# One-hots of the second expert index made token by token with partition scalars, and two weight remainders moved to VectorE

## The reference

```
q = (xt @ w_query).reshape(T, 8, 2, 128)          # two half queries per head
s_half, i_half = top_k(scores of both halves, 16)
top_s, pos = top_k(all sums of a first and a second half, 16)
ids = i_half[first] * 128 + i_half[second]         # expert (i, j) of 128 x 128
gates = softmax(top_s)
a = gelu(u_tab[ids] . x)                           # 128 experts a token
y = sum(gates * a * v_tab[ids])
```

## Time and profile before

| | us |
|---|---|
| median of 3 runs | 3461.05 (3458.17 to 3468.78) |
| the profiled execution | 3455.95 |
| its span | 3454.1 |
| PE busy | 3315.2 |
| DVE busy | 2983.2 |
| ACT busy | 2189.5 |
| POOL busy | 1302.3 |

### The profile page before, as it was taken

The page is one execution under the profiler, slowest core; times in us unless marked ns, Lnnn a source line. Parts: engine busy times, 40 slices in busy tenths (PEclk is TensorE's granted clock), DMA queues, the critical chain, the costliest instruction groups (busy, mean ns, idle before and its releaser), DMA issues.

```text
span 3454.1 us, 62688 instructions
## 1 busy us (share of the span) xinstructions
PE 3315.2 (96%) x19278; PEld 2433.7 (70%) x19278; DVE 2983.2 (86%) x6039; ACT 2189.5 (63%) x3116; POOL 1302.3 (38%) x1126
## 2 busy tenths in 40 slices
PE   6999999999999999999999999999999999999999
PEld 5777775667777767777777677766666777677777
DVE  6899877999888888888879997789988887888888
ACT  4574425557777677777746724455677776677777
POOL 0000017306555645555500000271255555556554
PEclk9999999999999999999999999999999999999999
DMA  5312263459999999999922123535699999999998
GB/s 201 104 58 71 92 256 104 154 180 327 365 362 342 341 364 360 361 351 358 337 90 88 56 80 122 213 117 177 213 326 346 356 338 349 366 364 355 359 354 303
DMA packets 421657, 868.79 MB, mean 252 GB/s; under 512 B 167824, under 2 KB 233360, under 8 KB 421008
## 3 DMA queue, kind: packets, MB, share of 16 engines
q1 hardware_dynamic: 310512, 544.87, 46.4%
q0 software_dynamic: 73728, 268.47, 21.4%
q10 hardware_dynamic: 37152, 52.45, 4.1%
HBM read 774.41 MB, written 85.98 MB: 249 GB/s over the span
## 4 chain that ended last, share of the span: by engine, by line
PE 43%; issue 26%; DVE 15%; POOL 10%; ACT 2%; DMA 2%; POOLq 0%; DVEq 0%; SPq 0%; ACTq 0%
PE ps L927 9%; PE ps L930 9%; PE ps L931 9%; POOL gbuf L589 6%; POOL spare L603 4%; PE ps L639 3%; PE ps L641 3%; PE ps L640 3%; DVE yT L1506 3%; DVE i L1752 2%; DVE v L1748 1%; DMA raw<-stream 1%; PE ps L673 1%; PE ps L674 1%; DVE S_ring L1758 1%
## 5 line engine op out<-in xcount | busy, mean ns | idle before, releaser
L673 PE MATMUL ps<-h,w 128*128 128x384 f16 (+1 forms) x2272 | 757.9, 334 | 34.0 <-ACT w L1015 33.2
L674 PE MATMUL ps<-h,w 128*128 128x384 f16 (+1 forms) x2272 | 754.7, 333 | 0.0
L1015 ACT ACTIVATE w<-w_hi 128x1024 f16<-128x1024 f32 x544 | 572.4, 1052 | 265.8 <-DVE w L1934 150.0
L603 POOL TENSOR_TENSOR spare<-spare 128x1 f32<-128x1 f32 x504 | 370.7, 735 | 908.7 <-DVE a_sp L1740 488.3
L930 PE MATMUL ps<-cf,w 128*128 128x384 f16 x2032 | 663.4, 327 | 0.0
L931 PE MATMUL ps<-cf,w 128*128 128x384 f16 x2032 | 660.7, 326 | 0.0
L670 PE MATMUL ps<-h_hi,w_hi 128*128 128x384 f32 (+1 forms) x2272 | 490.0, 357 | 0.0
L927 PE MATMUL ps<-cf_hi,w_hi 128*128 128x384 f32 x2032 | 428.4, 353 | 7.0 <-DVE cf L1928 7.0
L1934 DVE SCALAR_TENSOR_TENSOR w<-raw,w_hi 128x1024 f16<-128x1024 f32 x256 | 313.0, 1223 | 128.9 <-ACT w_hi L1010 99.6
L670 PEld LDWEIGHTS ps<-h_hi,w_hi 128*128 128x128 f32 x2272 | 396.1, 189 | 17.5 <-issue 0.3
L1003 ACT ACTIVATE w_hi<-raw 128x1024 fp32r<-128x1024 f32 x296 | 313.6, 1059 | 144.8 <-DMA raw<-stream 104.1
(11 more groups left out here) (285 smaller groups left out, 6227.4 us busy)
## 6 DMA issues: line engine op xcount, KB each, us to landing
raw<-stream SPq DMA_DIRECT2D x682, 512.0 KB
gelu_scratch<-g_out ACTq DMA_DIRECT2D x256, 192.0 KB
cg<-gelu_scratch SPq DMA_DIRECT2D x256, 192.0 KB
c_scratch<-stage SPq DMA_DIRECT2D x128, 256.0 KB
cg<-c_scratch SPq DMA_DIRECT2D x256, 128.0 KB
qT<-ada SPq DMA_DIRECT2D x32, 512.0 KB
cgate<-ada SPq DMA_DIRECT2D x32, 512.0 KB
w_rows<-ada SPq DMA_DIRECT2D x32, 512.0 KB
```

The costliest lines, as they stand in the source:

```text
L603: nc.gpsimd.tensor_tensor(spare[:, 16:17], spare[:, 17:18], spare[:, 18:19], ALU.add).then_inc(room, 1)
L673: nc.tensor.matmul(ps[:, b, 0:n], w16[:, s, 0, c], h16[:, c, 1, t0:T], start=False, stop=False)
L674: mm = nc.tensor.matmul(ps[:, b, 0:n], w16[:, s, 1, c], h16[:, c, 0, t0:T], start=False, stop=c == C - 1)
L1015: nc.scalar.mul(w16[:, s, 1], w_hi[:, s].bitcast(F32), X_DOWN).then_inc(w16_done, 1)
```

## The change

Three things. The j one-hots of a group are no longer made as a cube and multiplied: for each of the 8 tokens and each of the two gate parts, one DVE `tensor_scalar` compares a 128-column f16 row of numbers with the token's index, a per-partition f32 scalar, and multiplies by the gate, a second per-partition f32 scalar (16 instructions of 128 columns in place of three of 1024; the i one-hot stays). For this, indices and gates of j are kept in f32, a 128-column f16 row of numbers is made once at the start, and the gated tiles are stored token by token, so that PE reads them without gaps. The gate step of each 128 tokens gets two more instructions. Second, the remainders of query tiles 68 and 69 are made by DVE, after it has updated chunk 7 and before the second norm; POOL's first `low16` is then that of tile 70. Third, ACT's half words of tiles 68 and 69 stand behind the root in its queue. The semaphore between one-hot and gating goes, and the constants in POOL's waits follow.

```diff
--- before.py
+++ after.py
@@ -217,7 +217,8 @@
         cosT = keep("cosT", [P, T])
         sinT = keep("sinT", [P, T])
         ident16 = keep("ident16", [P, P], F16)
-        cur[0] += 960 - 256
+        iota16 = keep("iota16", [P, P], F16)
+        cur[0] += 960 - 512
         rstd_base = cur[0]
         rstd = keep("rstd", [P, T])
         sq_base = cur[0]
@@ -279,9 +280,11 @@
         esum = at("esum", base + 47 * KB, [P, 2, NB, RH])
         row_no = at("row_no", small + 6784, [P, 2, P])
         routed = at("routed", small + 8192, [P, NB, 3, RH * TOPK])
-        ij = at("ij", base + 64 * KB, [P, 2, ND], F16)
-        gate_hi = at("gate_hi", base + 64 * KB + 1536, [P, ND], F16)
-        gate_lo = at("gate_lo", base + 64 * KB + 2304, [P, ND], F16)
+        i_pick = at("i_pick", base + 64 * KB, [P, ND], F16)
+        j_pick = at("j_pick", base + 64 * KB + 768, [P, ND])
+        gate_hi = at("gate_hi", base + 64 * KB + 2304, [P, ND])
+        gate16 = at("gate16", base + 64 * KB + 3840, [P, ND], F16)
+        gate_lo = at("gate_lo", rstd_base, [P, ND])
         g_out = at("g_out", base + 68 * KB + 512, [P, 2, ND])
         sparse = base + 71 * KB + 512
         ids_u = at("ids_u", sparse, [P, P], U32)
@@ -291,9 +294,8 @@
         stage = at("stage", base, [P, 2, NKEYS, HALF])
         keys = at("keys", base + 74 * KB, [P, 2 * RH, NKEYS])
         one_i = at("one_i", base + 74 * KB, [P, 2, GROUP // 2, P, 2], F16)
-        one_j = at("one_j", base + 78 * KB, [P, 2, GROUP // 2, P, 2], F16)
-        gated_hi = at("gated_hi", base + 82 * KB, [P, 2, GROUP // 2, P, 2], F16)
-        gated_lo = at("gated_lo", base + 86 * KB, [P, 2, GROUP // 2, P, 2], F16)
+        gated_hi = at("gated_hi", base + 78 * KB, [P, 2, GROUP, P], F16)
+        gated_lo = at("gated_lo", base + 82 * KB, [P, 2, GROUP, P], F16)
 
         cg = at("cg", base + 74 * KB, [P, 4, NS + ND])
         coef = at("coef", base + 84 * KB, [P, 2, ND])
@@ -418,7 +420,6 @@
         id_r = sem("id_r")
         numbered = sem("numbered")
         gate_high = sem("gate_high")
-        j_done = sem("j_done")
         h_tr = sem("h_tr")
         h_ev = sem("h_ev")
         ids_in = sem("ids_in")
@@ -557,7 +558,7 @@
                 def low16(s, i):
 
                     high = pool.snap(l * NT + i + 1)
-                    up = pool.snap(l * (C * 2 + U_POOL) + i - I_QRY + 1)
+                    up = pool.snap(l * (C * 2 - 2 + U_POOL) + i - I_QRY - 1)
                     pool.wait_ge(hi_done, high)
                     nc.gpsimd.tensor_tensor(raw[:, s], raw[:, s], con[:, K_UP:K_UP + 1].rearrange("p (o q) -> p o q", o=1)
                                             .broadcast_to([P, C, P]), ALU.mult).then_inc(raw_up, 1)
@@ -569,10 +570,8 @@
                 nc.gpsimd.tensor_tensor(spare[:, 19:20], spare[:, 17:18], spare[:, 18:19], ALU.add)
 
                 nc.gpsimd.memset(uT[:, :, 0:PAD], 0.0).then_inc(pad0, 1)
-                pool.wait_ge(lo_done, l * NT + I_QRY + 4)
+                pool.wait_ge(lo_done, l * NT + I_QRY + 6)
                 nc.gpsimd.tensor_tensor(spare[:, 15:16], spare[:, 17:18], spare[:, 18:19], ALU.add)
-                low16(0, I_QRY)
-                low16(1, I_QRY + 1)
                 for c in range(C):
                     pool.wait_ge(hhi_done, (2 * l + 1) * C + c + 1)
                     nc.gpsimd.tensor_tensor(h16[:, c, 1], h_hi[:, c].bitcast(F32), con[:, K_ONE:K_ONE + 1].broadcast_to([P, T]),
@@ -895,9 +894,9 @@
                         for t in range(4):
                             two, k = 2 * q + t // 2, t % 2
                             cols = ps[:, 2 + (2 * g + q) % 4, t * P:(t + 1) * P]
-                            nc.tensor.matmul(cols, one_i[:, g % 2, two, :, k], gated_hi[:, g % 2, two, :, k],
+                            nc.tensor.matmul(cols, one_i[:, g % 2, two, :, k], gated_hi[:, g % 2, 4 * q + t],
                                              start=True, stop=False)
-                            mm = nc.tensor.matmul(cols, one_i[:, g % 2, two, :, k], gated_lo[:, g % 2, two, :, k],
+                            mm = nc.tensor.matmul(cols, one_i[:, g % 2, two, :, k], gated_lo[:, g % 2, 4 * q + t],
                                                   start=False, stop=True)
                         mm.then_inc(c_mm, 1)
 
@@ -1220,11 +1219,11 @@
                     if i == I_OUT + 2:
                         act.wait_ge(tile_done, l * NT + I_OUT + 4)
                         act.dma_start(keys[:], keys_d[ll]).then_inc(key_in, 16)
-                half_word_at(I_QRY)
                 updated_square(C - 1)
-                half_word_at(I_QRY + 1)
                 act.wait_ge(sq_used, l + 1)
                 token_root(7)
+                half_word_at(I_QRY)
+                half_word_at(I_QRY + 1)
                 modulated(1)
 
                 def half_scores_in(hp):
@@ -1324,6 +1323,7 @@
             for n, (counter, start) in enumerate(starts):
                 nc.vector.memset(spare[:, n:n + 1], 0.0).then_inc(counter, start)
             dve.wait_ge(rope_in, 32)
+            nc.vector.tensor_copy(iota16[:], iota)
             nc.vector.tensor_copy(numbers[:], iota.rearrange("k (n o) -> k n o", o=1).broadcast_to([P, P, 2])).then_inc(numbered, 1)
 
             steps = [0]
@@ -1698,6 +1698,11 @@
                                                        op0=ALU.add, op1=ALU.mult).then_inc(x_scaled, 1)
                         dve.wait_ge(x_scaled, l + 1)
                         nc.vector.tensor_scalar(gs[:, 1], gs[:, 1], X_UP, None, ALU.mult).then_inc(lay, 1)
+                for i in (I_QRY, I_QRY + 1):
+                    dve.wait_ge(hi_done, l * NT + i + 1)
+                    nc.vector.scalar_tensor_tensor(out=w16[:, i % 4, 0], in0=raw[:, i % 4], scalar=W_UP,
+                                                   in1=w_hi[:, i % 4].bitcast(F32), op0=ALU.mult,
+                                                   op1=ALU.subtract).then_inc(lo_done, 1)
                 norm(1)
 
 
@@ -1875,10 +1880,12 @@
                 for tt in range(1, NB):
                     dve.wait_ge(rt_tr, l * NBD + tt)
                     cols, gate = slice(P * (tt - 1), P * tt), ps[:, 2 + tt, 2 * P:3 * P]
-                    nc.vector.tensor_scalar(gate_hi[:, cols], gate, GATE_UP, None, ALU.mult).then_inc(gate_high, 1)
-                    nc.vector.tensor_copy(ij[:, :, cols], ps[:, 2 + tt, 0:2 * P].rearrange("k (c t) -> k c t", c=2))
+                    nc.vector.tensor_scalar(gate16[:, cols], gate, GATE_UP, None, ALU.mult).then_inc(gate_high, 1)
+                    nc.vector.tensor_copy(i_pick[:, cols], ps[:, 2 + tt, 0:P])
+                    nc.vector.tensor_copy(j_pick[:, cols], ps[:, 2 + tt, P:2 * P])
                     dve.wait_ge(gate_high, l * NBD + tt)
-                    nc.vector.scalar_tensor_tensor(out=gate_lo[:, cols], in0=gate, scalar=GATE_UP, in1=gate_hi[:, cols],
+                    nc.vector.tensor_copy(gate_hi[:, cols], gate16[:, cols])
+                    nc.vector.scalar_tensor_tensor(out=gate_lo[:, cols], in0=gate, scalar=GATE_UP, in1=gate16[:, cols],
                                                    op0=ALU.mult, op1=ALU.subtract).then_inc(rt_ev, 1)
                 dve.wait_ge(rt_ev, (l + 1) * NBD)
                 cube = [P, GROUP // 2, NKEYS, 2]
@@ -1891,13 +1898,13 @@
                     while lows[0] <= min(group_tile(g) + 1, NKEYS - 1):
                         u_low()
                     dve.wait_ge(c_mm, l * 2 * GROUPS + 2 * g + 2)
-                    nc.vector.tensor_tensor(one_j[:, g % 2], in_pairs.broadcast_to(cube), spread_out(ij[:, 1], g),
-                                            ALU.is_equal).then_inc(j_done, 1)
-                    nc.vector.tensor_tensor(one_i[:, g % 2], in_pairs.broadcast_to(cube), spread_out(ij[:, 0], g), ALU.is_equal)
-                    dve.wait_ge(j_done, l * GROUPS + g + 1)
-                    nc.vector.tensor_tensor(gated_hi[:, g % 2], one_j[:, g % 2], spread_out(gate_hi, g), ALU.mult)
-                    nc.vector.tensor_tensor(gated_lo[:, g % 2], one_j[:, g % 2], spread_out(gate_lo, g),
-                                            ALU.mult).then_inc(lr_done, 1)
+                    nc.vector.tensor_tensor(one_i[:, g % 2], in_pairs.broadcast_to(cube), spread_out(i_pick, g), ALU.is_equal)
+                    for gated, gates in ((gated_hi, gate_hi), (gated_lo, gate_lo)):
+                        for t in range(GROUP):
+                            n = GROUP * g + t
+                            ins = nc.vector.tensor_scalar(gated[:, g % 2, t], iota16[:], j_pick[:, n:n + 1], gates[:, n:n + 1],
+                                                          ALU.is_equal, ALU.mult)
+                    ins.then_inc(lr_done, 1)
                     while dots[0] < dots_by(g + 1):
                         dot()
                 while lows[0] < NKEYS:
```

## The result

| | before | after |
|---|---|---|
| median, us | 3459.6 (4 runs) | 3560.2 (3557.7 to 3563.5, 4 runs) |
| span of the profiled execution, us | 3454.1 | 3556.1 |

The ratio is 1.0278, 95% interval 1.026 to 1.0296: +96 us, +90 to +102. The forecast was 3535 us with a range of 3492 to 3600. The direction, the stage and the price of the new instruction held; a quarter of the loss was not in the sum.

What follows compares the result with a forecast made beforehand. PE was taken to bound the group stages, DVE having 1.1 to 1.3 us a group spare. Groups +78, gate step +1.3, row of numbers +0.2, norm -5.6: +74 on 3455.95, 3530; as median 3535 us, range 3492 to 3600.

Steps and rivals of the forecast that it cites:

- DVE becomes the bound of the group stage: Group stages: 16 short instructions, 3.58 us, replace 1.81, +1.78 us a group, more than DVE's spare time; together +78 us.
- the residual idle time, 9 us a layer: Group stages: idle time DVE would still have once it is the bound, added to the sum as 9 us a layer.
- the 2.1% of the first u tiles: DVE's idle share at 660 to 770 us, where it sets the pace; taken over for the group stages.
- rival B: Group stages: the ring DVE, PE, ACT, DVE keeps half of today's 110 us idle; +37 us, 3572 us, chance 0.10.
- the ring: Group stages: DVE, PE, ACT's copies and high part, DVE's remainder; 3.6 us around against 3.4 us of DVE work.
- PE's work stays at 382.7 us: Layer 1 group stage: PE's busy time of 382.7 us was to stay under 430, leaving PE room.
- Hidden up to 1.1 us a group, and beyond that DVE sets the end: Group stages: added DVE time up to 1.1 us a group costs nothing; beyond that, DVE sets the end.
- The second norm: With POOL quiet, DVE's four adds end sooner, chunk 7 is updated 2.8 us earlier, remainders nearly free; -5.6 us in all.
- rival D: Second norm: the change there gives nothing; 3541 us, inside the main case (0.60), with no chance of its own.
- A: Rival, group instructions: f16 gives at most two columns a cycle, step 0.258 us; +127 us, 3588 us, chance 0.17.
- C: Rival, group instructions: scalars hidden or short instructions cheaper, step 0.106 us, PE stays the bound; -4 us, 3457, chance 0.10.
- The gate step: Two PSUM reads and a cast replace one cast on DVE: +0.21 us three times a layer, +1.3 us in all.

Runs made afterwards that it cites:

- e5: The changed kernel with the gate of each token-wise instruction as a constant, leaving one partition scalar: 3495.7 us, ratio 1.0084 to the kernel before.
- e6: The changed kernel with both scalars of the token-wise instructions as constants, leaving out routing and gating: 3453.1 us, ratio 0.9964 to the kernel before.
- e7: The changed kernel comparing an f32 row of numbers in place of the f16 one: 3597.1 us, ratio 1.0383 to the kernel before.
- e4: The changed kernel with DVE's next remainder behind the group's dots instead of ahead of the group: 3527.4 us, ratio 1.0175 to the kernel before.
- e1: The kernel before with only the second norm's part changed (DVE's two remainders, half words behind the root): 3455.5 us, ratio 0.9972.
- e3: The kernel before, POOL starting its two remainders only after DVE's fourth add of squares, half words behind the root: 3456.4 us, ratio 0.9969.
- e8: e1 (groups as cubes) with the remainder order of e4: 3451.5 us, ratio 0.9964 to the kernel before.
- e2: The changed kernel with the second norm's part put back, leaving the groups' part alone: 3563.3 us, ratio 1.0281 to the kernel before.

## Why the prediction was right, and where it was short

- **DVE becomes the bound of the group stage: right.** The three numbers it was built from held: a fixed part of 0.07 us, 0.06 us a partition scalar, and 0.033 us for 128 f16 columns in place of 0.067 (e5, e6, e7). DVE's work came out at 420.0 us for 421.7.
- **The term that was too small: the residual idle time, 9 us a layer.** It was 23.2 and 17.5 us, 23 us more in all. From the sum's 74 us to the 102 between the two spans: +23 from this idle time, -4 from DVE's work, +9 from the rest of the kernel. The time is off by 25 and not by 28 because I added 5 us from the profiled execution to the median, and the changed kernel's is only 2 below its own. I took the 2.1% of the first u tiles, where DVE paces the kernel without such a ring. It was rival B's mechanism that came, given 0.10 and +37 us, and not half of the idle time stayed but 41 of 111 us. e4 takes it out and gets 35 us back, with 1.5% and 2.3% idle left, so 2.1% was about right for a DVE without the ring. That PE's work stays at 382.7 us did not hold either (395.6): the sum had no term for PE's clock falling where PE waits.
- **"Hidden up to 1.1 us a group, and beyond that DVE sets the end": wrong as a threshold.** From DVE's work, stage length and idle time of the group stages of layers 1 and 2, in us, one profiled execution each:

| kernel | step | DVE's work | stage | idle |
|---|---|---|---|---|
| e6 | 0.103 | 330.2, 330.1 | 387.6, 386.2 | 57.4, 56.1 |
| before | cubes | 338.0, 338.2 | 389.5, 397.4 | 51.5, 59.2 |
| e1 | cubes | 338.0, 337.9 | 394.2, 390.4 | 56.2, 52.6 |
| e5 | 0.164 | 375.2, 374.7 | 413.0, 408.7 | 37.8, 33.9 |
| after | 0.223 | 420.0, 419.9 | 443.2, 437.5 | 23.2, 17.5 |
| e7 | 0.256 | 444.6, 444.2 | 466.1, 455.3 | 21.5, 11.1 |

  From the kernel before to e5, 74 us of work in the two layers cost 35 us, though 111 were idle. Between kernels with the same cubes a stage differs by up to 7 us, so a single layer shows this only roughly, and whether the 8 us a layer between e6 and the cubes cost anything is not told: the stages say 11 to 13 us for both layers, the times of e6 and e1 are alike.
- **The second norm: right in mechanism.** -5.6 forecast, -7.1 by the traces' stretches, -10 (-6 to -14) by e1, so rival D (the norm gives nothing) is out. Chunk 7 came 2.7 and 2.1 us earlier where 2.8 was said; the surplus lies in PE's short steps behind it, which ran at a higher granted clock than before. Tile 67 was next, as said, and the remainders ended with the root (521.69 after 521.58). e3 shows the cause.
- **Rivals.** A is priced by e7: had the row of numbers run at two columns, +133 us (127 forecast). C (scalars hidden) falls with e5 and e6: its own step, 0.106, is what the instruction takes without scalars, and then the loss is gone, as it said. By the figure in the Trainium skill, "VectorE: DVE Perf Modes", section on the TRN2 errata, an instruction of this shape takes an estimated 94 ns, which is within a tenth of e6's 0.103 us and less than half of the 0.223 with two partition scalars.
- **The rest**: beside the stages' 94 us, the two spans differ by -1.6 ahead of the first group, +6.4 from the last group of layer 1 to the first of layer 2, and +3.6 behind. 1.8 in each of the last two is the last group's own instructions. The gate step took 1.1 us of it by the traces (1.3 forecast). What is left isn't explained by either part. From the last group of layer 1 to the first output chunk of layer 2 it is 1015.9 us in the kernel before and 1025.2 in the changed one, but 1019.9 to 1024.9 in e1, e3 and e8, which leave the groups as they were: the profiled execution of the kernel before was quick there.

## What to carry to other kernels

Price a short instruction by its step from start to start, and add its partition scalars: 16 instructions of 128 columns with two each cost twice what three of 1024 columns did, though they touch two thirds of the elements. An engine's idle time in a stage is not a budget: where its waits close a ring through other engines, part of the added work shows long before the engine is full (here 35 of 74 us, with 111 idle). And before moving work off an engine for its length, look at what ran beside it: here a wait in POOL's queue, with ACT's half words moved, gives the whole gain of the move.

## What the runs showed of the hardware

- A partition scalar costs 0.06 us each in DVE's queue (steps of 0.103, 0.164 and 0.223 us with none, one and two), not hidden by the instruction before.
- A TENSOR_SCALAR of 128 columns with f16 in and out takes 0.033 us less than with f32 in (steps of 0.223 and 0.256 us), which is 0.26 ns a column less.
- POOL's two-input operations slow DVE's two-input f32 adds from 0.68 to as much as 2.8 us (the kernel before); POOL's own (L565) took 2.73 us beside them and 2.35 with DVE all but quiet (e3).
- The granted clock of PE in the first group stage was 0.98 in the changed kernel, e2 and e4, 0.96 in e7 and 1.00 in the others. In the changed kernel it fell to the lower level (0.50) six times there, each time near the end of a wait of 2.5 us. Waiting for DVE does not bring this by itself: in e5 PE waited 24 us for it, 2.0 at the longest, at 1.00.
